# A two-block network in one kernel: column groups ended bank by bank, changed order at the stage entries, unread matmuls ahead of dense work

## The reference, cut to what matters

```python
def first_block(x, ...):
    h = rms_norm(x, norm_mix)
    z = h @ w_in                                   # 1024 x 3072
    y = concat([rms_norm(rglru_group(z)), hgrn2_group(z), rms_norm(moba_group(z))])
    x = x + y @ w_out
    h = rms_norm(x, norm_mlp)
    x = x + square(relu(h @ w_ff1)) @ w_ff2        # 4096 hidden features
    return rms_norm(x, norm_final)

def second_block(x, c, ...):
    shift1, scale1, gate1, shift2, scale2, gate2 = split(silu(c) @ w_ada + b_ada, 6)
    h = rms_norm(x, norm1_w) * (1 + scale1) + shift1
    q, k, v, r, a_lr, su, sv, g_a, g_b = split(h @ w_in, ...)   # 7184 columns
    merged = sigmoid(g_a) * gla(q, k, v, r, a_lr) + sigmoid(g_b) * sgu(su, sv)
    x = x + gate1 * (merged @ w_out)
    h2 = rms_norm(x, norm2_w) * (1 + scale2) + shift2
    x = x + gate2 * peer(h2, w_q, keys1, keys2, expert_down, expert_up)
    return rms_norm(x, final_norm_w)
```

## Time and profile before

| | |
|---|---|
| median of 3 runs | 1400.34 us (1400.04 to 1402.14) |
| the profiled execution | 1400.19 us |
| span of the profile | 1398.4 us |
| mean granted TensorE clock | 0.988 |
| TensorE matmuls (PE) | 97% of the span busy |
| GpSimd, VectorE, ScalarE | 75%, 56%, 51% |
| moved by DMA | 263.10 MB, mean 188 GB/s |

### The profile page before, as it was taken

The page is one execution under the profiler, slowest core; times in us unless marked ns, Lnnn a source line. Parts: engine busy times, 40 slices in busy tenths (PEclk is TensorE's granted clock), DMA queues, the critical chain, the costliest instruction groups (busy, mean ns, idle before and its releaser), DMA issues.

```text
span 1398.4 us, 27659 instructions
## 1 busy us (share of the span) xinstructions
PE 1354.7 (97%) x9252; PEld 1188.8 (85%) x9252; DVE 784.5 (56%) x1617; ACT 710.3 (51%) x1135; POOL 1054.8 (75%) x466
## 2 busy tenths in 40 slices
PE   7998999999999998999999999999999999999997
PEld 6887899998877886899999988888888888888886
DVE  4655433335256617249992288888877778411113
ACT  6354555555355444435556544444445555556663
POOL 6654688886678886768888877777767777888885
PEclk9999999999999999899999999999999999999999
DMA  8443677774545447535555554444444444565552
GB/s 322 143 172 117 228 296 271 280 276 149 198 138 196 136 165 285 202 136 181 180 180 182 178 179 163 168 160 170 162 152 172 165 165 166 177 246 193 194 195 90
DMA packets 72657, 263.10 MB, mean 188 GB/s; under 512 B 8208, under 2 KB 9104, under 8 KB 72224
## 3 DMA queue, kind: packets, MB, share of 16 engines
q1 hardware_dynamic: 72608, 262.46, 53.6%
HBM read 259.81 MB, written 2.62 MB: 188 GB/s over the span
## 4 chain that ended last, share of the span: by engine, by line
PE 88%; DVE 6%; ACT 2%; issue 2%; POOL 1%; DMA 1%; SPq 0%; POOLq 0%; ACTq 0%; DVEq 0%
PE bank L935 14%; PE bank L937 13%; PE bank L936 13%; PE bank L895 9%; PE bank L896 9%; PE bank L897 9%; PE bank L916 8%; PE bank L917 4%; PE bank L1365 3%; DVE arena L1858 1%; PE bank L920 1%; PE bank L1069 1%; POOL wlo L441 1%; DVE bank L1486 1%; PE bank L919 1%
## 5 line engine op out<-in xcount | busy, mean ns | idle before, releaser
L441 POOL TENSOR_TENSOR wlo<-raw,whi 128x1024 fp32r<-128x1024 f32 x432 | 1041.4, 2422 | 307.4 <-ACT whi L519 305.3
L519 ACT ACTIVATE whi<-raw 128x1024 fp32r<-128x1024 f32 x432 | 455.5, 1057 | 347.7 <-PE bank L937 257.9
L935 PE MATMUL bank<-whi,xhl 128*128 128x512 f32 x800 | 319.1, 399 | 11.8 <-POOL wlo L441 2.9
L895 PE MATMUL bank<-xhl,whi 128*128 128x256 f32 x1088 | 311.7, 286 | 8.0 <-DVE xhl L1439 3.4
L937 PE MATMUL bank<-whi,xhl 128*128 128x512 f32 x800 | 313.5, 392 | 0.0
L936 PE MATMUL bank<-wlo,xhl 128*128 128x512 f32 x800 | 312.7, 391 | 0.0
L896 PE MATMUL bank<-xhl,whi 128*128 128x256 f32 x1088 | 309.6, 285 | 0.0
L897 PE MATMUL bank<-xhl,wlo 128*128 128x256 f32 x1088 | 309.5, 284 | 0.0
L895 PEld LDWEIGHTS bank<-xhl,whi 128*128 128x128 f32 x1088 | 210.3, 193 | 12.8 <-issue 7.6
L896 PEld LDWEIGHTS bank<-xhl,whi 128*128 128x128 f32 x1088 | 210.5, 193 | 1.4 <-issue 0.2
L897 PEld LDWEIGHTS bank<-xhl,wlo 128*128 128x128 f32 x1088 | 210.4, 193 | 0.0
(11 more groups left out here) (311 smaller groups left out, 1468.5 us busy)
## 6 DMA issues: line engine op xcount, KB each, us to landing
raw<-stream SPq DMA_DIRECT2D x432, 512.0 KB, 3.3
arena<-ada SPq DMA_DIRECT2D x48, 512.0 KB, 4.6
arena<-rows SPq DMA_DIRECT2D x5, 512.0 KB, 8.8
xs<-x SPq DMA_DIRECT2D x2, 512.0 KB, 5.4
arena<-rows SPq DMA_DIRECT2D x1, 1024.0 KB, 5.4
x_spill<-xs SPq DMA_DIRECT2D x1, 1024.0 KB, 6.4
xs<-x_spill SPq DMA_DIRECT2D x1, 1024.0 KB, 6.7
out<-arena SPq DMA_DIRECT2D x2, 512.0 KB, 2.6
```

What stands on the lines that cost most here:

```text
L441: nc.gpsimd.tensor_tensor(wlo[:, slot, :], raw[:, slot, :], whi[:, slot, :].bitcast(F32), ALU.subtract).then_inc(lo_done, 1)
L519: nc.scalar.activation(whi[:, slot, :], raw[:, slot, :], ACT.Copy).then_inc(hi_done, 1)
L895: nc.tensor.matmul(dst, h_, xh[:, k, :], start=(k == 0), stop=False)
L935: nc.tensor.matmul(bank[b][:, :], ah[:, ts], whi[:, slot, cs], start=start, stop=False)
```

## The change

It changes the order of work at five places and adds matmuls whose result nobody reads.

**Added on TensorE.** `keep_warm(n, dst)` runs n matmuls of 512 columns over `uh` into a bank that the next work overwrites; `warm_up(n)` runs n 128x128 matmuls of ones (float32) into bank 5.

```diff
+            def keep_warm(n, dst):
+                for _ in range(n):
+                    nc.tensor.matmul(dst, uh[:, 0, 0:P], uh[:, :, :].rearrange("p a t -> p (a t)"), start=True, stop=True)
+            def warm_up(n):
+                pe.wait_ge(S("ones_set"), 1)
+                for _ in range(n):
+                    nc.tensor.matmul(bank[5][:, 0:P], ones, ones, start=True, stop=True)
```

```diff
-            sp.dma_start(xres[:, 0, :], x[:, 0:D]).then_inc(S("x_in0"), 16)
             tile(0, 0, None)
+            sp.dma_start(xres[:, :, 0:512], x_halves[:, :, 0:512]).then_inc(S("x_in0"), 16)
...
+            warm_up(16)
             pe.wait_ge(S("ident_in"), 16)
-            transposes("mix_T", "mix", xres)
+            for b in range(4):
+                if b == 2:
+                    warm_up(4)
+                pe.wait_ge(S(f"x_in{b // 2}"), 16)
...
+                if n == 1:
+                    f_tile(n, n + 1, bank[5][:, 0:T], ks=range(KC // 2))
+                    mix_row()
+                    f_tile(n, n + 1, bank[5][:, 0:T], ks=range(KC // 2, KC))
```

```diff
-            m_group(T_WOUT, "wout", "y", before=late_heads, within={3: att_turn})
+            m_group_by_banks(T_WOUT, "wout", 2, "y", before=late_heads, within={3: att_turn}, ahead=x1_turn_first,
+                             order=X1_ORDER)
...
-            turned_among("mlp", c_("mlp"))
+            x1_add(0)
+            x1_add(1)
+            turned_among("mlp", c_("mlp"), (0,))
+            x1_add(2)
+            turned_among("mlp", c_("mlp"), (1,))
+            x1_add(3)
+            turned_among("mlp", c_("mlp"), (2, 3))
```

```diff
-            for g in range(2, 8):
+            for g in range(2, 6):
                 ada_columns(g)
-            transposes("in2_T", "in2", xn)
+                keep_warm(2, bank[6][:, :])
...
             ada_row(8)
+            ada_columns(6)
+            keep_warm(3, bank[3][:, :])
             for n in range(2):
-                f_tile((T_IN2_F + n) % R, T_IN2_F + n + 1, bank[4 + n][:, 0:T], None if n else "in2")
+                f_tile_wide((T_IN2_F + n) % R, T_IN2_F + n + 1, bank[2 + n][:, :], None if n else "in2")
...
-                tsc(qk[:, n, :], bank[4 + n % 2][:, 0:T], 128 ** -0.5 if n < 4 else 1.0, None, ALU.mult)\
+                nc.vector.tensor_reduce(qk[:, n, :], bank[2 + n % 2][:, :].rearrange("p (a t) -> p t a", a=2), AX.X,
+                                        ALU.add).then_inc(S("qk_out"), 1)
```

```diff
-            m_group_by_halves(T_WOUT2, "wout2", 3, "merged", before=go_turn_rest)
+            m_group_by_banks(T_WOUT2, "wout2", 2, "merged", before=go_turn_rest)
...
-            transposes("wq_T", "wq", xn)
+            transposes("wq_T", "wq", xn, tts=(0,))
+            keep_warm(4, bank[5][:, :])
+            transposes("wq_T", "wq", xn, tts=(1,))
+            keep_warm(8, bank[5][:, :])
...
-                    f_tile(u, i * R + (T_WQ + R + u + 1), bank[4 + u % 2][:, 0:T])
+                    f_tile_wide(u, i * R + (T_WQ + R + u + 1), bank[4 + u % 2][:, :])
```

```diff
-            for banks in ((0, 1), (2, 3)):
-                for c in range(N_PEER - R, N_PEER):
-                    expert_m(c, None, final=(c == N_PEER - 1), banks=banks, used=banks == (2, 3))
+            expert_m(N_PEER - R, None)
+            for b in range(4):
+                for c in range(N_PEER - R + 1, N_PEER):
+                    expert_m(c, None, final=(c == N_PEER - 1), banks=(b,), used=b == 3)
```

More of the change, by code:

```diff
@@ L82, in acc_filled @@
     before = GROUPS[:GROUPS.index(group)]
-    return sum(4 if g in TRANSPOSES else 3 for g in before) + bank + 1
+    n = sum(4 if g in TRANSPOSES else 3 for g in before) + bank + 1
+    if group == "wout" and bank == 2:
+        return n + 2
+    return n - 1 if group == "mlp_T" and bank < 2 else n
 COLS = {}
@@ L539, in sums, with halves, upper_among @@
                     .then_inc(done, 1)
[L541 to L546 removed]
+            def halves(b, at=range(4)):
+                return [(2 * b + j, bank[at[b]][:, j * T:(j + 1) * T]) for j in range(2)]
+            def upper_among(group, gains, banks):
+                for b in banks:
                     act.wait_ge(acc_ready, acc_filled(group, b))
@@ L959, in m_group, with m_group_by_banks @@
                         part()
-            def m_group_by_banks(a, group, late, turned=None, before=lambda k: None, within={}, ahead=lambda b, k: None):
+            def m_group_by_banks(a, group, late, turned=None, before=lambda k: None, within={}, ahead=lambda b, k: None,
+                                 order=range(4)):
                 def tile(k, **kw):
@@ L976, in m_group_by_banks @@
                         tile(k, **kw)
-                for b in range(4):
+                for b in order:
                     for k in range(KC - late, KC):
@@ L986, in turn_of @@
                 for b in bs:
-                    pe.wait_ge(S(ready), 2 * tt + b // 2 + 1)
+                    read = 2 * tt + b // 2
+                    pe.wait_ge(S(ready), (X1_ORDER.index(read) if group == "mlp_T" else read) + 1)
                     if tt == 0:
@@ L996, in turn_of @@
                         last.then_inc(acc_ready, 1)
-            def m_group_by_halves(a, group, twice, turned=None, before=lambda k: None):
-                def tile(k, **kw):
-                    m_tile((a + k) % R, a + k + 1, xh[:, k, :], xl[:, k, :], final=(k == KC - 1), **kw)
-                for k in range(KC):
-                    before(k)
-                    if turned and k % 2 == 0:
-                        pe.wait_ge(S("turned_lo"), turn(turned, 4, k // 2 + 1))
-                    if k < KC - twice:
-                        tile(k, group=group if k == 0 else None)
-                    else:
-                        tile(k, banks=(0, 1), used=False)
-                for k in range(KC - twice, KC):
-                    tile(k, banks=(2, 3))
             def transposes(group, name, src, first=0, tts=range(TT)):
@@ L1779, in _, with x2_add @@
             own.sync()
-            for tt in range(TT):
+            both, small = s_(SS["sgm"]), s_(SS["sgv"])
+            def x2_add(tt):
                 for b in (2 * tt, 2 * tt + 1):
```

278 lines of the change are left out of this document (173 added, 105 removed).

## The result

The changed kernel takes 1387.6 us, median of 6 executions (1385.27 to 1391.01); the kernel before, in the 6 executions beside it, 1400.51 (1396.06 to 1402.14). The ratio is 0.9914, 95% interval 0.9892 to 0.9936: faster by 0.9%. The forecast was 1387.5. How much of that agreement is owed to the right reasons is what the rest is about.

A forecast was written before the change was run, and what follows sets the result against it. TensorE, busy 97% of the span, was taken as the bound, so only its standing still counted. Gains of 2.3 + 1.6 + 3.2 + 3.8 + 1.8 = 12.7 us took 1400.2 to 1387.5, range 1382.5 to 1394.0.

The forecast's parts named there:

- Parts 1, 2, 3 and 5: Start, output projection to MLP, MLP to second block, and the end: gains of 2.3, 1.6, 3.2 and 1.8 us.
- Part 1: The start: weights' tile 0 loaded ahead of x and split first, third tile starting near 18.5, not 20.86; gain 2.3 us.
- The clock at 14: Sign at the start: a granted clock of 1.00 at 14 us, where the kernel before showed 0.50.
- Part 2: Output projection to MLP: wout's tile 4 to the first row tile in 21.6 us, not 23.2; gain 1.6.
- Part 3: MLP to second block: dense work at 344.2, or 345.0 if the clock falls, against 347.30; gain 3.2 us.
- Part 4: Query projection: earlier dense work, first tile at full clock and wider tiles; gain 3.8 us, bounds -0.5 and 5.
- The first tile's 1.8: Query projection: its first tile takes 3.4 us instead of 5.2 at the fast clock, a gain of 1.8.
- A: Rival: unread matmuls don't hold the clock behind the MLP and at the queries, costing 4.6 us: 1392.1; chance 0.20.
- B: Rival: the stage entries stay late, the next wait eating the re-timings, 4.9 us back: 1392.4; chance 0.10.
- D: Rival: the entries don't change at all; only start, end and wide tiles gain, 5.2 us: 1395.0; chance 0.07.
- C: Rival: the unread matmuls are the bound, up to 19.8 us uncovered at the slow clock: 1407.3, slower; chance 0.02.
- the wide tiles: Second block's first projection and queries: tiles take 16 matmuls instead of 24, 2.80 us for 2.88; gain 1.1 us.

The follow-up runs named there:

- again_2: The changed kernel itself, unaltered, run once more: 1388.29 us, ratio to the kernel before 0.9907; its profile is of a 1391.58 us execution.
- fill_24: The changed kernel with 24 instead of 8 unread matmuls ahead of the first query tile: 1388.75 us, ratio to the kernel before 0.9912.
- only_start: The kernel before with the start's new order alone, without the warm-up matmuls: 1399.48 us, ratio to the kernel before 0.9990.

## Why the prediction was right, and where it was not

**The total is right, for about nine tenths of its reasons in size.** Parts 1, 2, 3 and 5 came as 2.36, 1.95, 2.99 and 2.04 against 2.3, 1.6, 3.2 and 1.8. That the median met the forecast within 0.1 us is luck: 1387.6 is the middle between 1386.06 and 1389.13, and no execution of the six lies there. All 16 executions of the changed kernel have a median of 1388.5, which is also 1400.2 less the 11.7 of the planned parts.

**Part 1.** The path was the one named: the low half of tile 0 at 5.26 (6.6 was forecast), sums of squares last, then the third tile's low half (the first of the two from 15.97, to about 18.35), and beside it VectorE's read of a bank, which ended at 18.38 and is what the wait is put down to; the `sil` multiply is off the path. Of the warm-up, "hidden, or up to 1 us" came out as hidden (32 passes from 1.06 to 6.48). The clock at 14 was named as a sign of the mechanism; it is none, as the third tile comes as early when dense work starts at double turns.

**Part 2** was undersized by 0.35. The two waits of 0.5 us in its sum, within the first MLP tile and ahead of the first row tile, were 0.22 (at 147.57) and 0.24 (at 155.74).

**Part 3.** Dense work began 3.2 us sooner relative to the first column, against 3.1 forecast. The moved final-norm scaling met a low half as the Trainium skill (SBUF — State Buffer, Who interferes with whom) has it: 2.78 us at 343.99 against 1.28 for the first one, and GpSimd's two passes beside them took 6.62 us, where two took 4.75 at 15.97. It was covered, as costed.

**Part 4 failed by one term.** "Stream tile 8 behind the spill lands one us ahead of its need: nothing, or 1 us": I took nothing, and it was a wait of 1.14. I had the right resource, the right tile and the right alternative, and chose the wrong end. The rows of SP's queue, first of the kernel before, then of the changed one:

```profile
566.14 0.43 SPq L412 DMA_DIRECT2D x_spill<-xs  x1
```

```profile
562.30 0.38 SPq L419 DMA_DIRECT2D x_spill<-xs  x1
...
571.12 12.93 SPq L343 DMA_DIRECT2D raw<-stream  x7
```

Against wout2's first tile the spill came 34.32 us behind before and 39.38 after: 5.1 later, and not 4. Dense work came 0.3 sooner than forecast. These two are 1.3 against a margin of one; the other 0.8 of the wait of 1.14 stays open. The start of dense work, 1.4 (32.84 to 31.46 behind wout2's first tile), was better than the 1.1 taken. The first tile's 1.8 was priced against the kernel before. Against the new order without fillers, the clock is worth 0.9. A query tile takes 2.82 at the fast level, for 2.80.

**The rivals.** A was not an alternative to the forecast but a part of the changed kernel's executions: 1391.6 at a clock of 0.993, near A's 1392.1, and 1385.3 at 0.999 are both this kernel. Against the first profile, A's two entries cost 4.1 there, for its 4.6. Its ground behind the MLP, that single-column passes let the clock fall and eight dense matmuls don't help, is what again_2 shows with TensorE busy throughout, and it should have had more than 0.20. B happened in part 4 alone, where the wait for a load took 1.14 back; D didn't. C needed all fillers uncovered; fill_24 shows that even 16 more cost 1.0.

**What was not seen** is that the kernel before has two more places with a falling clock, 1.6 us each, behind waits that nobody touched, and that they take part in every comparison. In the first profile they added 3.15 to a gain of 11.7; in the medians (12.9) some of it remains.

**What stays open.** Why the clock falls in one execution and holds in the next at the same place isn't settled by these runs; the start of the first transposes (6.5 to 8.0) shifts every later event, and only_start fits with a shift being enough, but one profile doesn't show it. No run has the new order of a single later entry (parts 2, 3 and 4), and none has the wide tiles without the new order or the order without them; their share (1.1 in the forecast) is seen only in the turns. A kernel with the fillers at the queries and ahead of the up tiles, the loads ahead, and nothing behind the MLP was not run.

## What to carry to other kernels

Judge unread matmuls against the same kernel without them, not against the old one: here the new order, with the wide tiles, gave all of the gain, and the fillers only a wider spread. The 16 executions of the changed kernel lie between 1385.3 and 1391.6, the 6 without fillers between 1387.2 and 1389.5. Fillers brought time in waits ahead of long dense work to which they were sized (a wait of 2.64 us at the experts, of 1.12 and 1.80 at the queries without them); they didn't among short passes with little idle time, where they ran at double turns when the clock fell all the same. When a stage becomes faster, look what in another queue was timed by its old pace: a load behind a spill that the change had moved back cost 1.14 us.

## What was not expected of the hardware

The clock fell behind identical waits in some executions and not in others: at the wait of 2.64 us ahead of the up tiles in eleven of the thirteen profiles that have it (not in the changed kernel's first and in fill_24's), worth 1.6 us each; at the wait of 2.04 us ahead of 446 in five of fourteen. It also fell with TensorE busy throughout, among single-column passes and 512-column matmuls (again_2 at 333). The mean clock that is listed with each execution tells its fastest from its slowest: for the changed kernel 0.999 goes with 1385.3 to 1386.1 us, 0.993 and 0.994 with 1391.0 to 1391.6.
